# The value products of a time-mix layer: computed in the mix stage, or spread over the steps of the pair recurrence

## The reference

```
def wkv7_scan(r, decay, k, v, kk, kka):   # S_t = S_{t-1} diag(w_t) - (S_{t-1} kk_t)(a_t kk_t)^T + v_t k_t^T ; y_t = S_t r_t
...
def rwkv7_time_mix(h, v_first, mu, w_in, w0, w1, w2, a0, a1, a2, k_k, k_a, r_k, lnx_w, lnx_b, w_out, v_res):
    ...
    r = xr @ w_in[0]
    k = xk @ w_in[1]
    v = xv @ w_in[2]
    g = xg @ w_in[3]
    w_log = -jax.nn.softplus(-(w0 + jnp.tanh(xw @ w1) @ w2).astype(f32)) - 0.5
    decay = jnp.exp(-jnp.exp(w_log))
    a = jax.nn.sigmoid((a0 + (xa @ a1) @ a2).astype(f32))
    ...
    y = wkv7_scan(rh, heads(decay), kh, vh, kk, kk * ah)
    y = head_group_norm(y, lnx_w.astype(f32), lnx_b.astype(f32))
    bonus = (jnp.sum(rh * kh * r_k.astype(f32), axis=-1, keepdims=True) * vh)
    y = (y + bonus.reshape(bsz, t, D_INNER)) * jax.nn.silu(g.astype(f32))
    return y.astype(h.dtype) @ w_out, v_first
```

## Time and profile before

| | us |
|---|---|
| median of 3 runs | 2113.08 (2111.18 to 2115.22) |
| the profiled execution | 2113.75 |
| its span in the trace | 2112.0 |

### The profile page before, as it was taken

How to read it: one execution, slowest core, us unless ns; L and a number is a source line. 1 busy time by engine, 2 the same in 40 slices (tenths; PEclk the granted TensorE clock), 3 DMA queues, 4 the chain that set the end, 5 groups by cost and what they waited for, 6 DMA issues and landing times.

```text
span 2112.0 us, 42671 instructions
## 1 busy us (share of the span) xinstructions
PE 2013.4 (95%) x16558; PEld 1629.3 (77%) x16558; DVE 1418.9 (67%) x2272; ACT 1008.1 (48%) x1765; POOL 174.7 (8%) x183
## 2 busy tenths in 40 slices
PE   5999999988888889999999999999999999999998
PEld 4877777777777776788888888888667778888886
DVE  7788888876666664555563655799786776445355
ACT  6666666645656665333232332442665434334243
POOL 5230000000233332200000000000000000000000
PEclk9999999999999999999999999999999999999999
DMA  4445555563333322233333333333113322333332
GB/s 121 122 143 164 168 178 183 178 139 74 94 74 75 89 59 82 80 90 99 99 96 98 95 99 90 100 90 100 50 41 100 100 70 81 99 95 95 100 92 78
DMA packets 395952, 215.19 MB, mean 102 GB/s; under 512 B 85136, under 2 KB 374312, under 8 KB 395816
## 3 DMA queue, kind: packets, MB, share of 16 engines
q1 hardware_dynamic: 395608, 213.18, 35.2%
q10 hardware_dynamic: 208, 0.06, 0.0%
HBM read 181.68 MB, written 31.52 MB: 101 GB/s over the span
## 4 chain that ended last, share of the span: by engine, by line
PE 86%; DVE 6%; ACT 3%; issue 3%; DMA 1%; SPq 1%; POOL 0%; DVEq 0%; ACTq 0%; POOLq 0%
PE bank L1911 23%; PE bank L1913 23%; PE bank L1912 23%; PE bank L596 3%; PE bank L573 1%; PE bank L604 1%; PE bank L506 1%; PE bank L547 1%; PE bank L520 1%; PE bank L1108 1%; PE bank L526 1%; ACT inv L821 1%; PE bank L539 1%; DVE inv L922 1%; PE bank L553 1%
## 5 line engine op out<-in xcount | busy, mean ns | idle before, releaser
L1911 PE MATMUL bank<-xl,w_hi 128*128 128x512 f32 x1568 | 615.7, 393 | 3.9 <-DVE xl L2633 2.5
L1912 PE MATMUL bank<-xl,w_lo 128*128 128x512 f32 x1568 | 611.1, 390 | 0.0
L1913 PE MATMUL bank<-xl,w_hi 128*128 128x512 f32 x1568 | 611.0, 390 | 0.0
L1558 ACT ACTIVATE w_hi<-w_raw 128x1024 fp32r<-128x1024 f32 x278 | 293.1, 1054 | 481.9 <-PE bank L1913 477.4
L2202 DVE TENSOR_TENSOR w_lo<-w_raw,w_hi 128x1024 fp32r<-128x1024 f32 x278 | 342.6, 1232 | 48.7 <-ACT w_hi L1558 40.0
L1911 PEld LDWEIGHTS bank<-xl,w_hi 128*128 128x128 f32 x1568 | 294.5, 188 | 76.6 <-issue 9.9
L1913 PEld LDWEIGHTS bank<-xl,w_hi 128*128 128x128 f32 x1568 | 294.8, 188 | 61.9
L1912 PEld LDWEIGHTS bank<-xl,w_lo 128*128 128x128 f32 x1568 | 294.9, 188 | 60.6 <-issue 0.5
L1911 PE MATMUL bank<-xh,w_hi 128*128 128x512 f32 x448 | 183.0, 409 | 10.9 <-DVE xh L2207 10.7
L1913 PE MATMUL bank<-xh,w_hi 128*128 128x512 f32 x448 | 175.5, 392 | 0.0
L1912 PE MATMUL bank<-xh,w_lo 128*128 128x512 f32 x448 | 175.4, 392 | 0.0
(11 more groups left out here) (385 smaller groups left out, 3165.5 us busy)
## 6 DMA issues: line engine op xcount, KB each, us to landing
w_raw<-in_a_w_in SPq DMA_DIRECT2D x64, 512.0 KB, 4.2
w_raw<-in_b_w_in SPq DMA_DIRECT2D x64, 512.0 KB, 4.1
w_raw<-in_w_ffn_up SPq DMA_DIRECT2D x42, 512.0 KB, 4.0
w_raw<-in_w_in SPq DMA_DIRECT2D x36, 512.0 KB, 3.8
w_raw<-in_a_w_out SPq DMA_DIRECT2D x16, 512.0 KB, 4.2
w_raw<-in_b_w_out SPq DMA_DIRECT2D x16, 512.0 KB, 4.0
w_raw<-in_w_ffn_down SPq DMA_DIRECT2D x16, 512.0 KB, 4.1
d_g<-sq SPq DMA_DIRECT2D x16, 256.0 KB, 2.2
```

Source lines behind the costliest of these rows:

```text
L1558: A(w_hi[0:rows, slot, 0:nkb, 0:ncol], w_raw[0:rows, slot, 0:nkb, 0:ncol], ACT.Copy).then_inc(s_hi, units)
L1911: mm(outp, wh, xlo, start=start, stop=False)
L1912: mm(outp, wl, xhi, start=False, stop=False)
L1913: return mm(outp, wh, xhi, start=False, stop=stop)
```

## The change

All sixteen value units leave the mix tiles. The first two (pair 0) are computed right behind the last mix tile, in banks 0 and 1; the other fourteen in turns 0 to 6 of the recurrence, two a turn for the pair of the next turn, both into bank 4 (`VALUE_BLOCKS`, `value_part`): a block of three matmuls behind the chain phase of each step 9 to 22, two blocks in steps 15 and 22. ACT copies a finished unit straight into `st_v` (`value_out`, steps 16 and 23), which SyncE spills from there (`spill_values`) and loads back for the bonus; the mix spills only the sum of the bonus (`bonus_copy`, `spill_bonus`), and GpSimd multiplies. To make room in memory `Y` changes places with `ra` and `bt`, its first ten tiles go to `d_y` from `yr` (`spill_y`) and come back in one transfer in turn 7, and `rhs` and `x_back` move.

The diff, cut to its core:

```diff
-U_OUT1 = U_MIX + 3 * CI
+U_VAL = U_MIX + 2 * CI
+U_OUT1 = U_VAL + CI
...
+        Y_STAGED = 5
+        VALUE_BLOCKS = {s: [(0, s - 9)] for s in range(9, 15)}
+        VALUE_BLOCKS[15] = [(0, 6), (0, 7)]
+        VALUE_BLOCKS.update({s: [(1, s - 16)] for s in range(16, 22)})
+        VALUE_BLOCKS[22] = [(1, 6), (1, 7)]
+
+        def values_read(p):
+            return U_VAL // 2 + p + 1
...
-                    pe.wait_ge(R["values_loaded"], LOAD_V * (t + 1))
+                    pe.wait_ge(R["decays_loaded"], LOAD_PC * (t + 1))
+                    for h in range(2):
+                        pe.wait_ge(s_free[h], values_read(t))
...
-                    if t == 0 and s == 1:
-                        pe.wait_ge(s_free[0], U_OUT1 // 2)
-                        pe.wait_ge(s_free[1], U_OUT1 // 2)
+                    if t == 1 and s == 0:
+                        pe.wait_ge(s_bonus, CI)
                     if when(t - 1, PAIRS):
                         chain(t - 1, s // 3, s % 3)
+                    if t + 1 < PAIRS:
+                        for a, k in VALUE_BLOCKS.get(s, ()):
+                            if (a, k) == (0, 0):
+                                if t == 0:
+                                    pe.wait_ge(s_n2m, CI)
+                                if t >= 2:
+                                    pe.wait_ge(R["y_rstd_made"], 2 * t - 2)
+                            if (a, k) == (1, 0):
+                                pe.wait_ge(s_free[0], values_read(t + 1))
+                            value_part(t + 1, a, k)
                     if t == PAIRS and s in OUT_BLOCKS:
...
+            def value_out(t, a):
+
+                act.wait_ge(s_unit, U_VAL + 2 * (t + 1) + a + 1)
+                act.wait_ge(s_vspill[a], 16 * (t + 2))
+                copy_values(a, bank[4])
...
+                    if s == 10 and when(t, PAIRS):
+                        out_weights(2 * t + 3 - CI)
+                    if s == 18 and when(t, PAIRS - 1):
+                        out_weights(2 * t + 4 - CI)
+                    if s == 16 and when(t, PAIRS - 1):
+                        value_out(t, 0)
...
+                            if 1 <= q <= Y_STAGED:
+                                act.wait_ge(s_yspill, 16 * (2 * q + 1))
...
+                    if s == 23 and when(t, PAIRS - 1):
+                        value_out(t, 1)
...
+                    if s == 11 and when(t, PAIRS):
+                        out_weights(2 * t + 3 - CI)
+                    if s == 19 and when(t, PAIRS - 1):
+                        out_weights(2 * t + 4 - CI)
...
+                o(G.tensor_tensor(st_bv[a][:], st_bv[a][:], st_bonus[a][:], ALU.mult))
...
+                where = yr[a][:] if q < Y_STAGED else Y[:, j, :]
...
-                panel(6 * t + (U_MIX + 3 * a + u), (a + u) % 2, w_in[(1, 0, 2)[u]], 0, KB, t * (2 * P) + a * P)
+                panel(4 * t + (U_MIX + 2 * a + u), u, w_in[1 - u], 0, KB, t * (2 * P) + a * P)
...
+            def spill_bonus(j):
+
+                sp.wait_ge(s_bonus, j + 1)
...
-            def mix_tile(t, a):
+
+            def mix_tile(t, a, first=False):
 
                 then = (t, 1) if a == 0 else (t + 1, 0)
                 mix_lora(*then)
                 mix(*then, 0)
                 mix(*then, 1)
+                if not first:
+                    spill_bonus(2 * t + a - 1)
                 spill_rates(t, a)
-                mix(*then, 2)
                 spill_rest(t, a)
 
...
+            def spill_values(p, a):
+
+                sp.wait_ge(s_free[a], values_read(p))
+                sp.dma_start(d_v[2 * p + a], st_v[:, a, 0:T]).then_inc(s_vspill[a], 16)
...
             sp.wait_ge(s_spill, SPILL_MIX + SPILL_TILE * (CI - 1))
-            sp.wait_ge(s_unit, U_MIX + 3 * (CI - 1) + 1)
+            sp.wait_ge(s_unit, U_MIX + 2 * (CI - 1) + 1)
             load_q(0, 0)
             load_keys(0)
-            sp.wait_ge(s_unit, U_MIX + 3 * (CI - 1) + 2)
-            load_values(0)
+            value_panel(U_VAL + 2)
             load_q(0, 1)
             spill_rates(CI // 2 - 1, 1)
             spill_rest(CI // 2 - 1, 1)
+            sp.wait_ge(s_unit, U_VAL)
+            load_decays(0)
             for half in range(2):
                 load_q(1, half)
-            panel(U_OUT1 + 1, 1, i["a_w_out"][0], 0, KB, P)
+            value_panel(U_VAL + 3)
+            spill_bonus(CI - 1)
+            for a in range(2):
+                spill_values(0, a)
             sp.wait_ge(s_spill, SPILL_MIX + SPILL_TILE * CI)
-            sp.wait_ge(s_unit, U_OUT1)
             for t in range(PAIRS + 1):
...
+                if t < PAIRS:
+                    value_panel(U_VAL + 2 * t + 4)
...
+                if t == PAIRS - 1:
+                    sp.wait_ge(s_yspill, 16 * (2 * Y_STAGED + 1))
+                    sp.wait_ge(s_unit, U_OUT1)
+                    sp.dma_start(Y[:, 0:2 * Y_STAGED, :],
+                                 d_y[0:2 * Y_STAGED].rearrange("k p t -> p k t")).then_inc(s_yback, 16)
...
-                w_high(n0 + 1, 1 - a, panels(U_MIX, 6, t, 3 * a + 1))
-                w_high(n0 + 2, a, panels(U_MIX, 6, t, 3 * a + 2))
+            def bonus_copy(j):
+                act.wait_ge(s_bon, j + 1)
+                A(o_bv[:], bank[5][:], ACT.Copy).then_inc(s_bonus, 1)
+
+            def mix(t, a, first=False, last=False):
+
+                j, n0 = 2 * t + a, 4 * t + (U_MIX + 2 * a)
                 act.wait_ge(s_kk, j + 1)
                 A(sqk[:], kk[:], ACT.Square).then_inc(s_sqk, 1)
-                if not (isinstance(j, int) and j < 1):
+                if not first:
                     act.wait_ge(s_bon, j)
                 A(sum_hi[:], kk[:], ACT.Square).then_inc(s_sqhi, 1)
+                if not first:
+                    bonus_copy(j - 1)
+                w_high(n0 + 2, 0, panels(U_MIX, 4, t, 2 * a + 2))
...
-                w_high(n0 + 3, 1 - a, panels(U_MIX, 6, t, 3 * a + 3))
+                w_high(n0 + 3, 1, panels(U_MIX, 4, t, 2 * a + 3))
...
-                act.wait_ge(s_unit, n0 + 3)
-                A(o_v[:], bank[a][:], ACT.Copy).then_inc(s_free[a], 1)
...
+            def copy_values(a, summed):
+                A(st_v[:, a, 0:T], summed[:], ACT.Copy)
+                A(st_v[:, a, T:T + C], summed[:, 0:C], ACT.Copy).then_inc(s_free[a], 1)
...
+            act.wait_ge(s_unit, U_VAL + 1)
+            copy_values(0, bank[0])
+            bonus_copy(CI - 1)
+            w_high(U_VAL + 2, 0, panels_by(U_VAL + 2))
+            act.wait_ge(s_unit, U_VAL + 2)
+            copy_values(1, bank[1])
+            recurrence_scalar(act, o, lambda n: w_high(U_OUT1 + n, n % 2, panels_by(U_OUT1 + n)), copy_values)
...
-                unit(n0, a, xl[0], free=free[0])
+                j, n0, free = 2 * t + a, 4 * t + (U_MIX + 2 * a), 2 * t + (U_MIX // 2 + a)
+                first = isinstance(j, int) and j < 1
+                unit(n0, 0, xl[0], free=free)
+                if not first:
...
-                unit(n0 + 1, 1 - a, xl[1], free=free[1])
-                if isinstance(j, int) and j < 1:
...
-                unit(n0 + 2, a, xl[2], free=free[2])
...
+            pe.wait_ge(s_xlo, X_Y)
+            unit(U_VAL, 0, xl[2], free=U_VAL // 2)
+            bonus(CI - 1)
+            unit(U_VAL + 1, 1, xl[2], free=U_VAL // 2)
...
+            def value_part(p, a, k):
+
+                n = U_VAL + 2 * p + a
+                if k == 0:
+                    pe.wait_ge(s_lo, n + 1)
+                last = three(bank[4][:], w_hi[:, a, k, :], w_lo[:, a, k, :], xl[2][:, 0, k, :], xl[2][:, 1, k, :],
+                             k == 0, k == KB - 1)
+                if k == KB - 1:
+                    last.then_inc(s_unit, 1)
...
-                w_low(n0 + 1, 1 - a)
...
-                w_low(n0 + 2, a)
...
+                w_low(n0 + 2, 0)
...
-                dve.wait_ge(s_bon, j + 1)
-                dve.wait_ge(s_free[a], 3 * t + (FREE_MIX + (3 * a + 2) // 2 + 1))
-                V.tensor_tensor(o_bv[:], o_v[:], bank[5][:], ALU.mult).then_inc(s_fin, 1)
```

More of the change, by code:

```diff
@@ L248, in program @@
         head_mean = over("head_mean", [P, P])
+        st_bonus1 = over("st_bonus1", [P, T])
         assert spot <= xh_at
         spot = xh_at
-        Y = over("Y", [P, CI, T])
+        ra, bt = [], []
+        for n in range(2):
+            ra.append(over(f"ra{n}", [P, 2, NCH, 2, C]))
+            bt.append(over(f"bt{n}", [P, 2, NCH, P]))
         assert spot == big_at
-        x_back, _, _ = place("x_back", [P, NT, D], F32, big_at + 2 * 32768)
+        x_back, _, _ = place("x_back", [P, NT, D], F32, xh_at)
         st_q = [over(f"st_q{n}", [P, 2, NCH, 3, C]) for n in range(2)]
@@ L262, in program @@
         st_pc = [over(f"st_pc{n}", [P, 2, NCH]) for n in range(3)]
+        rhs = over("rhs", [P, 2, C])
         assert spot <= big_at + 2 * 32768
         spot = big_at + 2 * 32768
-        ra, bt = [], []
-        for n in range(2):
-            ra.append(over(f"ra{n}", [P, 2, NCH, 2, C]))
```

(46 more changed lines are left out.)

97 lines of the change are left out of this document (58 added, 39 removed).

## The result

The changed kernel takes 2219.15 us (median of 4 runs, 2217.08 to 2220.14) against 2112.13 (median of 4, 2108.9 to 2115.22): a ratio of 1.0506, 95% interval 1.0487 to 1.0524. It is slower by 5%, as forecast (2214). The profiled execution took 2218.69 us with a span of 2217.0, so the two traces differ by 105.0 us.

A forecast was written before the change was run, and what follows sets the result against it. TensorE was taken to bound the mix before, a late panel in the VectorE chain after. Mix +20.0, way in +8.7, first turn +10, six turns +62, reload +0.5 give +101: 2214 us, range 2188 to 2242, chance 0.80.

The forecast's parts named there:

- The sign: Whole kernel: slower 0.97, within about 4 us of no change 0.01, faster 0.02.
- Rival (a): Mix: the panel lands in time after all, a tile takes 16.0 us, the kernel 2154 us; chance 0.08.
- The term of the mix: Mix tiles: ScalarE waits for a late panel, 20.1 us a tile against 18.5; +20.0 us in all.
- the way in: From last mix tile to first recurrence transposes: loads wait for the bonus spill, +3.6, then the decay load, +5.1; +8.7 us.
- turn 7: Last inversion turn: loading back 2.5 MB of spilled Y tiles may slow instruction loads, +0.5 us.
- the first turn: First recurrence turn, which has no chain: moved products less the idle time they fill, taken as +10 us.
- turns 1 to 6: Six recurrence turns: +10.3 us each from 14.0 of blocks plus waits, less 5.4 of idle time filled; +62 us.
- the wait for bank 4: Step 16 of a turn: PE idles 1.7 to 1.9 us until ACT has copied the first value unit out.
- the 0.5 of L547: Step 23 of a turn: PE's wait of 0.5 us disappears under the double block of step 22.
- The 0.3 in step 9: Step 9 of a turn: a wait of 0.3 us for the norm's scale, which ACT reads from the same bank.
- rival (b): Clock: one half-clock stretch in each turn with the new wait, 2228 us, chance 0.08; mix cold throughout, 2298, 0.02.
- Rival (c): Inversion steps: instruction supply alone sets the pace, products run in time already paid; with mix at 16.0, 2091 us; chance 0.02.

The follow-up runs named there:

- the three repairs: Changed kernel with the key panels issued earlier, first value unit finished in step 14 to free bank 4, and the decay load issued earlier: 2136.78 us, 1.0099 of the kernel before.
- The small reload: Changed kernel with one of the ten spilled Y tiles loaded back in the last inversion turn, the other nine filled with zeros: 2213.8 us.
- the early one: Y reloaded about 20 us earlier, on a kernel with early panel and decay load, bank wait removed, o_b, o_c and receptance low weights on GpSimd: 2148.95 us, 1.016.

## Why the prediction was right

**The sign and the size** come from two of its terms, and both held. It said that the mix would get slower though 76 us of products left it, because ScalarE would stand before a panel that SyncE issues after the last spill: 20.1 us a tile was worked out, 20.1 was measured, with the wait of about 4 us that it named (4.47), and the run with the early panel took away wait and cost together, to 15.84 where 16.0 was worked out. Rival (a) was priced at 2154 for this case; the kernel in which it was made true took 2154.29. That the two agree so closely is luck: on its own chip this kernel is 44.3 us above the one before, and the rival's price is 41 above. The term of the mix was 1.8 us short, all of it in the first tile (20.2 us for 18.3), where the panel was issued 0.4 us later than in the row of before and landed 4.8 us after its issue, for 4.2; the other fourteen took 281.4 us, 20.1 each.

That the whole came within 4 us (105.0 for 101) owes something to luck too: the mix, the way in and turn 7 were put too low by 9.0 us together, the first turn and turns 1 to 6 too high by 5.4.

**The way in** was mis-sized by 3.3 us. The term was the landing of the bonus spill, 2.8 us by the row of before: it now stands behind two panels and needed 5.0 (issued at 440.66; the first load, which waits for it, is issued at 445.71), so the first load came at kk + 7.5 and not + 5.3. In the run where the spill goes ahead of the panels it took 2.3 us (441.58 to 443.91). The other 1.1 us lie between the first load and the transposes, 20.6 us where 19.6 were forecast. SyncE's rows there, in after:

```profile
438.70 1.18 SPq L1347 DMA_DIRECT2D w_raw<-in_a_w_in  x2
440.66 0.65 SPq L1391 DMA_DIRECT2D d_bv<-o_bv  x1
445.71 1.32 SPq L1448 DMA_DIRECT2D st_q<-d_q  x2
```

That PE's two units would set the start if the order let them was right, but the 4 us put on it were too few: in the run with the early decay load they set the start, and the stretch is 8.5 us longer than before, in the three repairs 6.6.

**The turns.** Six turns grew by 58.4 us, forecast 62. PE's work grew by 80.4 us (252.0 to 332.4), 13.4 a turn for the 14.0 of the blocks; stops at "issue" fell from 28.3 us in these six turns to none, 4.7 a turn; the wait for bank 4 is 9.7, 1.6 a turn against 1.7 to 1.9; the 0.5 of L547 went. 13.4 - 4.7 + 1.6 - 0.5 = 9.8, and 9.7 a turn was measured. The 0.3 in step 9 did not show. That a little over 5 us of idle time would fill held only with all the products in: the runs with fewer had stops left and a lower clock, and one unit alone cost 6.9 us a turn over before, two 9.7. The prediction also put the roundings, corrections and transfers of the turns at nothing; in the changed kernel that came out, and in the runs without products it did not.

**Turn 7** was mis-sized: 0.5 for the reload, 4.4 measured. The step said that the spilled tiles "may slow instruction loads", and took too little: the turn has no products to cover the stops, which are 6.9 us there against 3.5 in the kernel before, and the 2.5 MB fell into its inversion steps (issued 890.46, landed 902.87). The small reload and the early one both take 4 to 5 us back.

**The clock.** Where PE is idle for about 5 us a tile, nearly all in one wait, the granted clock of the mix is 0.84; it is 1.00 where the early panel leaves 2 us idle and no wait of PE above 1.1. That agrees with the rule of the Trainium skill (TensorE: Matmul & The Clock Gate, Why this matters for your kernels) that idle gaps between matmul bursts bring the half clock back. It cost the mix nothing here: DVE takes each kk without a wait for PE. In the turns the clock was 1.00 in four of the six and 0.97 in two, with the bank wait in all six, so rival (b) did not come true. Rival (c) needed turns that cost less than 4.4 us; they cost 9.7.

## What to carry to other kernels

Before work is moved out of a stage because its engine is full, work out the second bound and what the other engines wait for there: here the stage could give back 2.7 us of the 5.5 that each unit takes, and gave back none, since a transfer issued late came to stand in the chain. Idle time that is made of many short stops takes work, but at a price (about 14 us of products for 4.7 of idle time), and a wait that is taken away may come back as such stops where nothing covers them. Loads that are ordered by one queue should be placed by the time at which they are needed, a wait of a spill ahead of a load included.
